# A two-block transformer on one core: residual stream with tokens on partitions, norms by statistics passes, six projections with stationary tokens

## The reference

```python
def first_block(...):
    h = modulate(rms_norm(x, norm1_g), shift1, scale1)       # h * (1 + scale) + shift, one pair per feature
    hc = modulate(rms_norm(xc, norm1_g), cmods[0], cmods[1])  # 256 context tokens
    y, yc = token_mixer(h, hc, P, last)                       # ends in m @ w_out
    x = x + gate1 * y
    h = modulate(rms_norm(x, norm2_g), shift2, scale2)
    return x + gate2 * grouped_moe(h, router_w, router_b, moe_w_gate, moe_w_up, moe_w_down)

def second_block(...):
    for i in range(2):
        y = mixer_ab(x, ...) if i % 2 == 0 else mixer_c(x, ...)   # both end in @ w_out
        x = layer_norm(ALPHA * x + y, ln_mix_g[i], ln_mix_b[i])
        f = conv_ffn(x, ...)                                      # (gelu(conv(x @ w_gate)) * (x @ w_up)) @ w_down
        x = layer_norm(ALPHA * x + f, ln_ffn_g[i], ln_ffn_b[i])
        x = x + sigmoid(x @ ple_w_gate[i]) * (p[i] @ ple_w_proj[i])
```

## Time and profile before

| what | us |
|---|---|
| median of three runs | 1888.32 (1881.66 to 1894.05) |
| the profiled execution, device time | 1890.97 |
| its span in the profile | 1889.2 |
| TensorE busy in matmuls | 1693.1 |
| VectorE busy | 1112.9 |
| ScalarE busy | 893.2 |
| GpSimd busy (starting loads) | 5.5 |

### The profile page before, as it was taken

One profiled execution on the slowest core, in us unless ns is written; L12 is line 12 of the kernel. 1 busy time (PEld: TensorE's weight loads), 2 busy tenths in 40 slices (PEclk: granted clock), 3 DMA queues, 4 the chain that ended last, 5 costly groups with the idle time before them and its releaser, 6 DMA issues.

```text
span 1889.2 us, 25575 instructions
## 1 busy us (share of the span) xinstructions
PE 1693.1 (90%) x11052; PEld 1502.8 (80%) x11052; DVE 1112.9 (59%) x1308; ACT 893.2 (47%) x1039; POOL 5.5 (0%) x13
## 2 busy tenths in 40 slices
PE   2988799998999599999989988989998997899997
PEld 1486686877999578777989946789997985799997
DVE  3765546252456658787555575556555657465555
ACT  3353425361533467676435334554445536454534
POOL 0000000000000000000000000000000000000000
PEclk8899898986999789999999979999999998899999
DMA  9244330210753169998645503235544450255540
GB/s 332 89 134 134 100 112 1 91 54 17 239 185 134 68 230 371 324 366 320 215 159 179 162 31 134 69 108 203 178 160 154 165 170 23 90 175 184 177 156 23
DMA packets 137127, 293.69 MB, mean 155 GB/s; under 512 B 5079, under 2 KB 16520, under 8 KB 136440
## 3 DMA queue, kind: packets, MB, share of 16 engines
q1 hardware_dynamic: 135504, 286.88, 44.2%
q10 hardware_dynamic: 968, 3.66, 0.5%
q0 software_dynamic: 544, 1.52, 0.3%
HBM read 291.00 MB, written 1.05 MB: 155 GB/s over the span
## 4 chain that ended last, share of the span: by engine, by line
PE 79%; DVE 11%; ACT 7%; DMA 2%; issue 1%; SPq 0%; POOL 0%; ACTq 0%; DVEq 0%
PE bank L408 78%; DVE cut L1212 2%; ACT cut L1985 2%; DMA raw<-in_w_mod 1%; PE bank L421 1%; ACT pairs L1991 1%; DVE stat L1394 1%; ACT arena L2151 1%; DVE arena L1225 1%; DVE pairs L1220 1%; ACT arena L2065 0%; DVE arena L1233 0%; DMA arena<-in_positions 0%; DVE arena L1273 0%; DVE arena L1389 0%
## 5 line engine op out<-in xcount | busy, mean ns | idle before, releaser
L408 PE MATMUL bank<-pairs,cut 128*128 128x256 f32 (+1 forms) x8016 | 985.7, 286 | 53.7 <-DVE pairs L1220 34.0
L408 PEld LDWEIGHTS bank<-pairs,cut 128*128 128x128 f32 (+1 forms) x8016 | 975.9, 193 | 64.7 <-issue 42.2
L1212 DVE TENSOR_TENSOR cut<-raw,cut 128x2048 fp32r<-128x2048 f32 x273 | 613.5, 2260 | 425.8 <-ACT cut L1985 425.3
L1985 ACT ACTIVATE cut<-raw 128x2048 fp32r<-128x2048 f32 x273 | 513.0, 1888 | 396.4 <-PE bank L408 353.0
L408 PE MATMUL bank<-cut,pairs 128*128 128x512 f32 (+1 forms) x1212 | 282.4, 394 | 8.8 <-DVE pairs L1220 7.9
L408 PEld LDWEIGHTS bank<-cut,pairs 128*128 128x128 f32 x1212 | 226.1, 193 | 58.4 <-issue 9.6
L408 PE MATMUL bank<-arena 128*128 128x128 f32 (+10 forms) x748 | 203.4, 442 | 42.9 <-DVE arena L1340 9.6
L408 PEld LDWEIGHTS bank<-arena 128*128 128x128 f32 (+4 forms) x748 | 124.9, 221 | 100.6 <-issue 72.2
L408 PE MATMUL bank<-arena,cst 128*128 128x256 f32 (+5 forms) x248 | 91.5, 508 | 19.6 <-ACT arena L2373 6.7
L1991 ACT ACTIVATE pairs<-arena 128x256 fp32r<-128x256 f32 (+1 forms) x91 | 43.6, 510 | 101.4 <-DVE arena L1892 51.4
L408 PE MATMUL bank<-cut,sct 128*128 128x512 f32 x192 | 57.2, 458 | 35.6 <-DVE cut L1212 35.6
(11 more groups left out here) (243 smaller groups left out, 849.8 us busy)
## 6 DMA issues: line engine op xcount, KB each, us to landing
raw<-in_moe_w_gate SPq DMA_DIRECT2D x32, 1024.0 KB, 7.0
raw<-in_moe_w_up SPq DMA_DIRECT2D x32, 1024.0 KB, 6.5
raw<-in_moe_w_down SPq DMA_DIRECT2D x32, 1024.0 KB, 6.6
raw<-in_w_in SPq DMA_DIRECT2D x30, 1024.0 KB, 5.4
raw<-in_w_mod SPq DMA_DIRECT2D x24, 1024.0 KB, 5.4
raw<-in_ffn_w_gate SPq DMA_DIRECT2D x22, 1024.0 KB, 5.1
raw<-in_ffn_w_up SPq DMA_DIRECT2D x22, 1024.0 KB, 5.1
raw<-in_ffn_w_down SPq DMA_DIRECT2D x22, 1024.0 KB, 4.9
```

The costliest lines, as they stand in the source:

```text
L408: return pe.matmul(o, l, r, start=start, stop=stop, skip_group_check=True)
L1212: v.tensor_tensor(both[:, PIECE:PIECE + n], M.raw[i % RAW][:, 0:n], both[:, 0:n].bitcast(F32), ALU.subtract).then_inc(*up("lo_w", i))
L1985: a.activation(M.cut[K.slot(i)][:, 0:n], M.raw[i % RAW][:, 0:n], ACT.Copy).then_inc(*up("hi_w", i))
```

## The change

`XT` now has 128 tokens on partitions, two blocks of 1024 features. Nine norms or hand-overs change with it.

- A norm takes its statistics within a partition: for the RMS norms a square with a sum on ScalarE (`roots_of`), for the layer norms `bn_stats` and `bn_aggr` on VectorE. A reciprocal of one column and one multiply (`over_root`, `over_deviation`) follow. Then TensorE turns the two blocks with 16 transposes (`turn_block`), and ScalarE reads the transposed banks, applies weight and bias per partition, and cuts as before. All `sums` across partitions of the stream are gone.
- `w_out`, both output projections, the down projections of the experts and of both feed-forward networks, the side projection and the gate of `p` go through `rows`: a token tile is stationary and 512 weight columns are streamed into a block (i, q) of 128 tokens and 512 features. These were 2496 matmuls of 256 columns and are 1248 of 512; `scatter` changes from 48 to 24.
- The gates of the stream vary along the free axis now: `spread_row` copies chunks 4, 5, 10 and 11 over all partitions with one matmul each, in place of their columns.
- The layer norm's result with weights along the free axis is needed for the residual too. GpSimd computes it: a load of a row of weights, then per block a multiply and an add of 128x1024.
- The gather takes normed tokens before scale and shift, one product in place of two; ScalarE applies scale and shift after it.
- Where no norm stands between (the stream after the experts, `x2`, and after the first layer, `x3`), the blocks are turned as well, and both cuts read the bank.

The core of the diff:

```diff
+        if c not in (4, 5, 10, 11):
+            late.append(c)
+
+    def turn_block(key, src, among=Q, parts=1, name=None):
+
+        outs = [claim(("tr", key, j), ("lo", name, j) if name else ("mo", key, j), among) for j in range(4)]
+        for i in range(2) if parts == 1 else (0,):
+            for j in range(4):
+                for b in (i,) if parts == 1 else (0, 1):
+                    P.wait_ge(*(at("xn", key, b) if parts == 1 else at("xn", key, b, j // 2)))
+                    for t in range(2):
+                        m, x = 2 * j + t, t * 256 + b * 128
+                        last = turned(outs[j][:, x:x + 128], src[:, b, m * 128:m * 128 + 128])
+                if i == 1 or parts == 2:
+                    last.then_inc(*up("tr", key, j))
+
+    def rows(key, w, X, nk, r0, tile, ready, first, last_, free, among, order, place=None, label=None):
+
+        for k0 in range(0, nk, 2):
+            h = take(w, r0 + k0, 2, 0, 1024, place=place)
+            for n, (i, q) in enumerate(order):
+                if first and k0 == 0:
+                    claim(("rw", key, i, q), free(i, q), (among[2 * i + q],))
+                for k in range(2):
+                    P.wait_ge(*at(*ready(k0 + k)))
+                    t, c = slice(128 * i, 128 * i + 128), slice(512 * q, 512 * q + 512)
+                    x = tile(k0 + k)
+                    last = mm3(bank[among[2 * i + q]][:, :], (X.hi[:, x, t], X.lo[:, x, t]), (h.hi[:, k, c], h.lo[:, k, c]),
+                               first and k0 + k == 0, last_ and k0 + k == nk - 1)
+                if last_ and k0 + 2 == nk and n < 3:
+                    last.then_inc(*up("rw", key, i, q))
+            if k0 + 2 < nk:
+                leave(h, last)
+            elif last_:
+                leave(h, last, "rw", key, *order[3])
+            else:
+                leave(h, last, *label)
+
+    def spread_row(c, among):
+
+        o = claim(("gr", c), ("G", c), among)
+        P.wait_ge(*K.load("brow", 1 + c // 8))
+        P.wait_ge(*at("mrow", c))
+        x = 512 * (c % 2)
+        mm(o[:, :], C("fold")[0:5, 0:1].broadcast_to([5, 128]), M.mrow[0:5, x:x + 512], True, True).then_inc(*up("gr", c))
...
             P.wait_ge(*K.load("dft"))
             P.wait_ge(*at("PM", o_))
             chain(o[:, :], [(M.DFf[:, i, c0:c0 + 128], M.PM[:, s, i, o_, :]) for i in range(2)]).then_inc(*up("hf", o_, j))
-    sums(("rx",), ("rmsq", "x"), M.SQ, lambda j: ("sq", "x", j))
+    turn_block("x", M.XN)
     mod_chunk(3)
-    sums(("rc",), ("rmsq", "c"), M.SQ, lambda j: ("sq", "c", j))
     mod_columns()
 
...
+    turn_block("c", M.XC)
...
-
-
-    sums(("r2",), ("rmsq", "2"), M.T1, lambda j: ("sq", "2", j))
-    H2S, H2T, EX = M.H2S, M.H2T, ("moe_w_gate", "moe_w_up", "moe_w_down")
+    for c in (4, 5):
+        spread_row(c, Q)
+    BLOCKS, HALVES = [(0, 0), (0, 1), (1, 0), (1, 1)], [(0, 0), (1, 0), (0, 1), (1, 1)]
+    rows("wo", D["w_out"], M.HM, 8, 0, lambda k: k, M.HM.ready, True, True, lambda i, q: ("wor", i, q), Q, BLOCKS)
+
+
+    held[0] = ("mod", 1)
+    turn_block("2", M.T1)
...
-                chain(o[:, 0:384], [(x[:, i, k * 128:k * 128 + 128], M.P[:, i, :])
-                                    for i in range(2)]).then_inc(*up("gx", name, k))
+            o = claim(("gx", k), ("fg", k), (2, 3, 4, 5, 6, 7))
+            chain(o[:, 0:384], [(x[:, i, k * 128:k * 128 + 128], M.P[:, i, :])
+                                for x in (H2T.hi, H2T.lo) for i in range(2)]).then_inc(*up("gx", k))
...
-                for s in range(3):
                     for x in (M.Y[s].hi, M.Y[s].lo):
-                        last = mm(o[:, t * 256:t * 256 + 256], x[:, m // 4, (m % 4) * 128:(m % 4) * 128 + 128],
-                                  M.BACK[:, s, :], (t, s) == (0, 0) and x is M.Y[s].hi, False)
+                        last = mm(o[:, :], M.BACK[:, s, i * 128:i * 128 + 128], x[:, q, :], s == 0 and x is M.Y[s].hi, False)
         last.then_inc(*up("scat"))
...
+    turn_block("x2", M.XT, parts=2, name="XS0")
...
     def layer_norm(i, which, hook=None):
-        sums(("ln1", i, which), ("mean", i, which), M.T1, lambda j: ("T1" + "mf"[which], i, 2 * j))
         if hook:
             hook()
-        sums(("ln2", i, which), ("rmsq", ("ln", i, which)), M.XT, lambda j: ("sq", ("ln", i, which), j))
+        turn_block(("ln", i, which), M.T1)
...
+    def over_root(key, X, XN, i):
+
+        rs = M.cols(("rs", key), 2)[:, i:i + 1]
+        w(*at("std", key, i))
+        v.reciprocal(rs, rs).then_inc(*up("v"))
+        w(*at("v"))
+        v.tensor_scalar(XN[:, i, :], X[:, i, :], rs, None, ALU.mult).then_inc(*up("xn", key, i))
...
+    def second_parts(name, F, dst):
+
+        for j in range(4):
+            cut_lo(name, j, dst.lo[:, 2 * j:2 * j + 2, :], F[:, 2 * j:2 * j + 2, :], dst.hi[:, 2 * j:2 * j + 2, :])
...
-                                       op1=ALU.add).then_inc(*(up("dnx", i) if m % 2 else up("v")))
-        if i:
-            j = slice(2 * i - 2, 2 * i)
-            cut_lo("XS0", i - 1, M.XS.lo[:, j, :], M.XT[:, j, :], M.XS.hi[:, j, :])
+    for q in range(2):
+        for i in range(2):
+            x, y = slice(512 * q, 512 * q + 512), M.T1[:, i, 512 * q:512 * q + 512]
+            w(*at("G", 10 + q))
+            w(*at("rw", "dn", i, q))
+            v.tensor_tensor(y, M.bank[2 * i + q][:, :], M.G2[:, x], ALU.mult).then_inc(*up("dnr", i, q))
+            w(*at("dnr", i, q))
+            v.tensor_tensor(M.XT[:, i, x], M.XT[:, i, x], y, ALU.add).then_inc(*up("xn", "x2", i, q))
+
+    def turned_parts(key, name, dst):
+
+        for j in range(4):
+            src = M.bank[K.bank("tr", key, j)][:, :].rearrange("p (j t) -> p j t", j=2)
+            w(*at("hi", name, j))
+            v.tensor_tensor(dst.lo[:, 2 * j:2 * j + 2, :], src, dst.hi[:, 2 * j:2 * j + 2, :].bitcast(F32),
+                            ALU.subtract).then_inc(*up("lo", name, j))
+
+    turned_parts("x2", "XS0", M.XS)
...
+    def layer_norm(i, which, key_in, dst):
+
         key = ("ln", i, which)
-        mean, rms = M.SRb[:, 256:512], M.SRb[:, 0:256]
-        w(*at("ln1", i, which))
-        v.tensor_scalar(mean, M.bank[K.bank("ln1", i, which)][:, 0:NT], 1.0 / 1024, None,
-                        ALU.mult).then_inc(*up("mean", i, which))
-        w(*at("mean", i, which))
-        for j in range(0, 8, 2):
-            x = M.T1[:, j:j + 2, :]
-            v.tensor_tensor(x, x, wide(mean, 2), ALU.subtract).then_inc(*up("cen", key, j // 2))
-        invert(key, rms)
-        w(*at("rms", key))
-        for n in range(5):
-            j = 2 * n
-            if n < 4:
-                x = M.T1[:, j:j + 2, :]
-                v.tensor_tensor(x, x, wide(rms, 2), ALU.mult).then_inc(*up("t1", key, n))
-            if n:
-                c = slice(j - 2, j)
-                cut_lo(dst, n - 1, M.XS.lo[:, c, :], M.XT[:, c, :], M.XS.hi[:, c, :])
+        BN = M.cols("bn_stats", 24).rearrange("p (i n) -> p i n", i=2)
+        MV = M.cols("bn_aggr", 4).rearrange("p (i n) -> p i n", i=2)
+        rs = M.cols(("rs", "ln"), 2)
+
+        def sums(b):
+            for q in range(2):
+                x = M.XT[:, b, 512 * q:512 * q + 512]
+                w(*at("rw", key_in, b, q))
+                if which:
+                    w(*at("xr", ("ln", i, 0), b))
+                v.scalar_tensor_tensor(out=x, in0=x, scalar=ALPHA, in1=M.bank[K.bank("rw", key_in, b, q)][:, :],
+                                       op0=ALU.mult, op1=ALU.add).then_inc(*up("z", key, b, q))
+                w(*at("z", key, b, q))
+                v.bn_stats(BN[:, b, 6 * q:6 * q + 6], x).then_inc(*up("v"))
+            w(*at("v"))
+            v.bn_aggr(MV[:, b, :], BN[:, b, :]).then_inc(*up("var", key, b))
+
+        def over_deviation(b):
+            w(*at("std", key, b))
+            v.reciprocal(rs[:, b:b + 1], rs[:, b:b + 1]).then_inc(*up("v"))
+            w(*at("v"))
+            if which or i:
+                w(*at("xr", ("ln", i, 0) if which else ("ln", 0, 1), b))
+            v.tensor_scalar(M.T1[:, b, :], M.XT[:, b, :], MV[:, b, 0:1], rs[:, b:b + 1], ALU.subtract,
+                            ALU.mult).then_inc(*up("xn", key, b))
+
+        sums(0)
+        sums(1)
+        over_deviation(0)
+        over_deviation(1)
+        second_parts(dst, M.MX, M.XS)
...
-            v.tensor_tensor(x, x, g, ALU.add).then_inc(*up("xo", i, m))
-            if i == 0:
-                cut_lo("XC2", m // 2, M.XC2.lo[:, m:m + 2, :], x, M.XC2.hi[:, m:m + 2, :])
+        for q in range(2):
+            for b in range(2):
+                g, x = M.SGM[:, b, 512 * q:512 * q + 512], M.XT[:, b, 512 * q:512 * q + 512]
+                w(*at("pga", i, b, q))
+                w(*at("rw", ("pp", i), b, q))
+                v.tensor_tensor(g, g, M.bank[2 * b + q][:, :], ALU.mult).then_inc(*up("pgm", i, b, q))
+                w(*at("pgm", i, b, q))
+                w(*at("xr", ("ln", i, 1), b))
```

(36 more changed lines are left out.)

385 lines of the change are left out of this document (171 added, 214 removed), and 2 rows, old and new, of the table SHARED.

## The result

The changed kernel takes **1894.11 us** (median of 20 runs, 1889.55 to 1899.09); the kernel before takes 1884.07 in 20 runs (1880.57 to 1894.05). The ratio is 1.0046, with an interval of 1.0034 to 1.0059: half a per cent slower, where 1.5% faster was forecast. The two profiled executions are close to each other (1891.99 after, 1890.97 before), because the latter lay 6.9 us above its own median.

A forecast was written before the change was run, and what follows sets the result against it. TensorE, busy 1693 of 1889 us, was taken as the bound. Terms 8.6 + 22.6 + 8.5 + 4.4 - 2.8 - 5.3 - 3.0 = 33.0 off 1890.97 gave 1858.0, corrected by 2.65 to 1855.3, stated as 1856; range 1844 to 1874.

The forecast's parts named there:

- What they cost the path is the harm they do ... I take 3: GpSimd's 16 passes in the layer norms: delay to VectorE's multiply and low parts beside them, a loss of 3 us.
- The first rival: Layer norms: GpSimd and VectorE keep each other out, 2.45 us a pass, 11.4 us in four norms, 1864; chance 0.28.
- the norm after a network: Two layer norms: gate projection at T (preceding projection's last matmul ends) + 10.2 instead of 20.8; 22.6 us for both.
- The rate, 8.5 us: Projections through `rows`: 1248 matmuls of 512 columns at 230.4 ns replace pairs of 256 at 238.3, gaining 8.5 us.
- The layer norms: Four norms, two after output projections and two after networks: shorter chains ahead of TensorE, gaining 8.6 and 22.6 us.
- the first kind: Two layer norms after output projections: network starts 10.6 us after the projection's last matmul instead of 14.9; 8.6 us together.
- a sign of being wrong: Layer norms: prediction wrong if the weight cut ends after the high part, or a statistics pass exceeds 1.5 us.
- Norm of the first input: Conditioning chunk's chain: second sum of ones, 3.69 us, goes and a multiply of 0.69 leaves; gain 4.4 us.
- Hand-over after the experts: Turning the stream after the experts, no norm between: TensorE's wait of 2.45 us grows to T + 5.3; minus 2.8.
- After the first layer: Hand-over to the next layer: gate projection no longer follows without a gap, T + 5.3 again; minus 5.3 us.
- Second norm and routing: Low parts and transposes leave the routing chain, the gather slows to ScalarE's pace; nil, -4 to +4 us.
- The context's norm: Norm of the context: its transposes come behind banks VectorE still reads; between -1 and +2 us, taken as nil.

The follow-up runs named there:

- e3: The changed kernel with GpSimd's affine pass of each layer norm held back until VectorE's fourth low part is done; 1868.35 us, 0.9910 of before.
- e2: The changed kernel with tile `stat` 656 columns wide instead of 640, arena 64 bytes higher at 131872; 1881.29 us, 0.9985 of before.
- e4: The changed kernel with both edits, GpSimd's affine pass held back and the arena at 131872; 1859.51 us, 0.9865 of before.
- e15: The changed kernel, GpSimd's passes not held back, with `stat` at 664 columns and the expert stage's tiles 56 columns up; 1858.26 us, 0.9874 of before.
- e13: e5 with the bank order of e7 and the expert stage's tiles 56 columns up; 1836.47 us, 0.9748 of before.
- e7: e4 with the four blocks of the gate projection's first piece in the order in which ScalarE gives back the banks; 1855.58 us.
- e1: The kernel before with only `stat` widened from 400 to 640, so the arena starts 960 bytes higher; 1905.4 us, 1.0116 of before.
- e14: The kernel before with the arena at 130880 and the expert stage's tiles 56 columns up; 1861.95 us, 0.9884 of before.
- e12: The changed kernel, GpSimd's passes not held back, with `stat` at 664 columns and the expert stage's tiles 24 columns up; 1863.82 us, 0.9895 of before.
- e10: The kernel before with `stat` at 408 columns (arena at 130880) and the expert stage's tiles 24 columns up; 1863.17 us, 0.9896 of before.
- e8: e4 with each layer norm's affine pass moved from GpSimd to VectorE, behind its four low parts; 1858.66 us.
- e16: e3 with `stat` at 680 columns, the arena at 131968; one run, 1861.11 us.
- e6: e3 with `stat` at 648 columns, the arena at 131840; 1861.83 us, 0.9883 of before.
- e11: e5 with the cut weights moved up by 64 bytes and the arena unchanged at 131904; 1861.74 us, 0.9885 of before.
- e5: e3 with `stat` at 664 columns, the arena at 131904; 1837.17 us, 0.9762 of before.

## Why the prediction was wrong

The forecast was 1856. Its baseline was the median of three runs, 1888.3; over 20 runs it is 1884.1, so its 33 us of gain meant 1851. The measured 1894 is 43 away from that. Two things account for most of it, and only the first has a term in the sum. Point by point:

1. **The step that failed: "What they cost the path is the harm they do ... I take 3".** GpSimd's passes cost 25.8 us (e3), 21.8 at the place of before (e2 to e4), and 21.8 at the best place (e15 to e13, e7's order in it). The first rival named the mechanism and got its pass right (2.45 us; 2.35 measured), but it was given a chance of 0.28 and only 11.4 us. The multiply and the low parts were held as it says. What it left out: in the norm after a network the cut of weights and the low part are caught too, not the multiply alone (T + 15.7 against T + 9.7 for the first gate matmul, so 6 us a norm instead of 2.1). In the other norm it is T + 16.3 against T + 10.6, 5.7 instead of 3.6.
2. **The step that was not there: the place.** No term covered what a wider tile does to the addresses behind it. It costs the changed kernel 12.8 us (e2; 8.8 once GpSimd is late), and the kernel before 20 (e1).
3. **The rate, 8.5 us, had the wrong upper row.** The steps' 230.4 ns was read as what `rows` would reach, because it loads and alternates alike. It was their place: in e4 `rows` comes at 233.4, and at 228.9 in e13, where its operands lie as those of the steps do. A pair of 256 was 237.4 (two of 118.7), not 238.3, so in e4 a pair gains 4 ns and 1248 pairs 5.0 us (1.5 where 256 columns come at 117.3). At the changed kernel's own place (234.2) it is 4.0. At distance 192 a pair takes 226.8 or 235.6 ns and one of 512 takes 228.9: on the faster level the wide form loses. The Trainium skill, "TensorE: Matmul & The Clock Gate", section "Wait — 56ns, not 53.3ns?", has one fixed cost of about 2.5 ns per matmul. Two of 256 less one of 512 would show it: 4.0 ns at distance 160, minus 2.1 at 192. The runs decide, and here it isn't one number.
4. **The layer norms were right once GpSimd was away**: T + 10.6 in e4 for the first kind, forecast T + 10.6; T + 9.7 for the first gate matmul, forecast 10.2, then 1.5 us lost to a bank that ScalarE still reads (e7), which wasn't foreseen. A statistics pass is 0.695 us, the multiply 0.81 (0.76 taken); the cut ahead of the low parts cost 0.4. It ended later than the high part, which the prediction had named as a sign of being wrong: by 0.4 in e4, and by 2.1 in the changed kernel.
5. **The small terms held.** Norm of the first input, from the start of the run ahead of the conditioning chunk to the first projection: 43.5 us in place of 49.0, plus 5.5 (4.4 forecast). Hand-over after the experts: T + 4.8, where 2.45 was before, minus 2.4 (2.8 forecast). After the first layer: 1483.1 to 1488.4, minus 5.3 (5.3). Second norm and routing, from the end of the first block's output projection to the first slot matmul: 55.1 us in place of 56.2, plus 1.1 (nil, -4 to +4). The context's norm, from the start of one projection to that of the next: 109.1 in e4, 108.0 before, minus 1.1 (nil).

GpSimd 19 more than allowed, the place 13, the rate 3.5, the bank 3 and the context's norm 1 are 39.5 of the 43. But what came out better than forecast (the first input 1.1, the hand-over 0.4, the second norm 1.1, two gate projections 0.5 each) adds 3.6 to what has to be explained, so some 7 us have no cause shown.

Is the change itself worth anything? That depends on the place. At distance 160 it is 0.15% faster than before (e2, interval to 1.0000). At 192 it is 0.2% faster (e15 beside e14, 3.7 us) or 0.7 us slower (e12 beside e10), with intervals that overlap: no difference that can be told at either. At 96 it is 11.3 us faster: 1.0046 (1.0034 to 1.0059) beside e1's 1.0116 (1.0091 to 1.0140), intervals that lie apart. There two of 120.0 ns give way to one of 234.2, which for 1248 pairs comes to 7 of the 11 us (estimate). With GpSimd late it is worth 1.35% (e4), and 25 us at the best place (e13 beside e14; e7's order is in it, and one network of e14 was at its slower rate). The fastest version is e13, 48.7 us below the kernel before; about half of that is places alone (e14, 23.2 us), which have nothing to do with the change.

## What to carry to other kernels

When a change gives work to an idle engine, price it by what its neighbour does in that microsecond: GpSimd's passes beside VectorE's chain held two VectorE operations ahead of the first matmul in one kind of norm and three in the other, by some 2 us each, and the same passes begun behind VectorE's last low part cost no more than VectorE doing them itself (e8 beside e4). When a change resizes or adds a tile, note how far apart the two operands of the most frequent matmuls lie before and after, and move them back before the rest is judged; run the old kernel with the new layout as a control. A rate read in another place of the trace is a bound only if its operands lie alike.

## What the runs showed of the hardware that was not expected

- The time from one split matmul to the next depends on the distance between cut activations and cut weights, taken modulo 256 bytes, with no change of an instruction: 256 columns at 113.3 to 120.3 ns, 512 columns at 226.7 (e16) to 234.4. The distance that is best for 256 columns streamed from the activations (192) isn't the best for 512 columns streamed from the weights (0 in e16). The 0 does not rest on that one run alone: the cut context tokens lie 128 bytes further than the stream, so at 0 in e6 and e11, and their part of a projection with 512 columns streamed comes at 226.6 to 229.3 ns there, beside 231.7 to 233.3 for the stream at 128. The float32 matmuls did not move: those that read one operand from the arena and one from the constants have a median of 429 to 431 ns for 512 columns, before and in e1, e4, e5, e6, e11 and e16. What in the memory makes it so isn't settled.
- At one place there are still two levels, 113.4 and 117.8 ns at distance 192, 117.3 and 118.7 at 160. e14 shows both in one execution, in its two networks of the same instructions, 188.58 and 182.93 us. Steps of 512 columns have two levels as well at distance 128: e1 has both, 16.73 and 16.80 us for 72, in one execution. What chooses between them stays open. It may be why single runs of one kernel range so far (e14 over 14.5 us), which was not tested.
- VectorE and GpSimd take turns in both directions: beside VectorE's cuts GpSimd's pass takes 4.3 to 4.5 us in place of 2.4.
